# The sum of squares of three norms by four 32-column products, a copy and one product inside a column

## What is computed

```python
def rmsnorm(x, g):
    x32 = x.astype(jnp.float32)
    y = x32 * lax.rsqrt(jnp.mean(x32 * x32, axis=-1, keepdims=True) + EPS)
    return (y * g.astype(jnp.float32)).astype(x.dtype)
...
    a = rmsnorm(h, norm2[i])                                      # norm 2
    h = h + (jax.nn.silu(a @ w_gate[i]) * (a @ w_up[i])) @ w_down[i]
...
def sq_relu_mlp(h, w_up, w_down):
    return jnp.square(jax.nn.relu(h @ w_up)) @ w_down
...
    x = x + sq_relu_mlp(rmsnorm_2(x, mlp_norm[layer]), w_up[layer], w_down[layer])   # layer 0 and 1
```

## Time and profile before

| | |
|---|---|
| median of 3 runs | 887.29 us |
| lowest of them | 886.36 us |
| the profiled execution | 886.04 us, of it the span 884.3 us |
| granted TensorE clock, mean | 0.998 |
| TensorE busy | 868.6 us |
| weight loads | 837.4 us |
| VectorE busy | 607.5 us |
| ScalarE busy | 470.6 us |
| GpSimd busy | 95.0 us |

### The profile page before, as it was taken

How to read it: one execution, slowest core, us unless ns; L and a number is a source line. 1 busy time by engine, 2 the same in 40 slices (tenths; PEclk the granted TensorE clock), 3 DMA queues, 4 the chain that set the end, 5 groups by cost and what they waited for, 6 DMA issues and landing times.

```text
span 884.3 us, 19363 instructions
## 1 busy us (share of the span) xinstructions
PE 868.6 (98%) x7310; PEld 837.4 (95%) x7310; DVE 607.5 (69%) x994; ACT 470.6 (53%) x755; POOL 95.0 (11%) x139
## 2 busy tenths in 40 slices
PE   8999999999999999999999999999999999999996
PEld 8888899999999999787999999999999999999996
DVE  4766558666566587877866666668979966666665
ACT  6556666434444385448744444445786644444443
POOL 3420002000000029611100000001110100000001
PEclk9999999999999999999999999999999999999999
DMA  7532336665655648623465555555534565555551
GB/s 250 170 118 97 118 122 223 204 191 173 204 177 181 198 147 234 175 98 125 160 225 189 183 187 187 189 188 166 166 131 158 169 214 189 189 188 185 188 174 48
DMA packets 44434, 152.10 MB, mean 172 GB/s; under 512 B 5604, under 2 KB 6884, under 8 KB 44388
## 3 DMA queue, kind: packets, MB, share of 16 engines
q1 hardware_dynamic: 41184, 145.52, 50.3%
q0 software_dynamic: 2400, 4.89, 1.8%
q10 hardware_dynamic: 804, 1.04, 0.3%
HBM read 148.64 MB, written 1.05 MB: 169 GB/s over the span
## 4 chain that ended last, share of the span: by engine, by line
PE 87%; DVE 7%; ACT 3%; issue 1%; DMA 1%; SPq 0%; DVEq 0%; ACTq 0%
PE bank L1363 26%; PE bank L1365 26%; PE bank L1364 26%; DVE alo L953 2%; DVE wlo L929 2%; PE bank L1713 1%; PE bank L1397 1%; PE bank L1447 1%; PE bank L1492 1%; PE bank L1469 1%; PE bank L1803 1%; ACT whi L513 1%; DMA raw<-in_slabs 1%; DVE h L963 1%; PE bank L1391 1%
## 5 line engine op out<-in xcount | busy, mean ns | idle before, releaser
L1363 PE MATMUL bank<-ahi,whi 128*128 128x256 f32 (+1 forms) x1400 | 400.4, 286 | 1.9 <-DVE alo L947 1.2
L1364 PE MATMUL bank<-alo,whi 128*128 128x256 f32 (+1 forms) x1400 | 394.0, 281 | 0.0
L1365 PE MATMUL bank<-ahi,wlo 128*128 128x256 f32 (+1 forms) x1400 | 393.9, 281 | 0.0
L929 DVE TENSOR_TENSOR wlo<-raw,whi 128x1024 fp32r<-128x1024 f32 x273 | 332.2, 1225 | 30.3 <-ACT whi L513 30.2
L513 ACT ACTIVATE whi<-raw 128x1024 fp32r<-128x1024 f32 x273 | 282.4, 1051 | 93.1 <-PE bank L1365 83.4
L1363 PEld LDWEIGHTS bank<-ahi,whi 128*128 128x128 f32 x1400 | 264.0, 189 | 6.4 <-DVE alo L947 2.6
L1364 PEld LDWEIGHTS bank<-alo,whi 128*128 128x128 f32 x1400 | 264.0, 189 | 0.4
L1365 PEld LDWEIGHTS bank<-ahi,wlo 128*128 128x128 f32 x1400 | 264.3, 189 | 0.0
L1363 PE MATMUL bank<-hidhi,whi 128*128 128x256 f32 x704 | 195.1, 277 | 0.7 <-DVE hidlo L947 0.7
L1365 PE MATMUL bank<-hidhi,wlo 128*128 128x256 f32 x704 | 195.1, 277 | 0.0
L1364 PE MATMUL bank<-hidlo,whi 128*128 128x256 f32 x704 | 194.4, 276 | 0.0
(11 more groups left out here) (223 smaller groups left out, 724.4 us busy)
## 6 DMA issues: line engine op xcount, KB each, us to landing
raw<-in_slabs SPq DMA_DIRECT2D x273, 512.0 KB, 3.5
shared<-in_convw POOLq DMA_DIRECT2D x4, 512.0 KB, 6.8
shared<-zpad POOLq DMA_DIRECT2D x48, 35.5 KB, 3.6
raw<-in_slabs SPq DMA_DIRECT2D x8, 128.0 KB, 5.4
vtok<-in_gatew POOLq DMA_DIRECT2D x2, 512.0 KB, 5.4
out<-y SPq DMA_DIRECT2D x4, 256.0 KB, 2.8
h<-in_xT ACTq DMA_DIRECT2D x3, 272.0 KB, 5.2
h<-in_xT SPq DMA_DIRECT2D x1, 272.0 KB, 3.5
```

Source lines behind the costliest of these rows:

```text
L929: dve.tensor_tensor(wlo[:, n % R, :, :], raw[:, n % R, :, :], whi[:, n % R, :, :].bitcast(F32), ALU.subtract).then_inc(lo_done, 1)
L1363: pe.matmul(dst, hi, xh, start=start, stop=False, skip_group_check=True)
L1364: pe.matmul(dst, hi, xl, start=False, stop=False, skip_group_check=True)
L1365: return pe.matmul(dst, lo, xh, start=False, stop=stop, skip_group_check=True)
```

## The change

For the three norms `N_NORM2`, `N_MLP0` and `N_MLPC` (the table `PARTS`), the four products with 128 columns of ones are replaced. TensorE now multiplies each of GpSimd's four sums by 32 columns of ones, each product into 32 partitions of its own of half 1 of `stat_bank` (`stats_parts`). ScalarE copies the 128x256 result into `sq` 1 (`parts_factor`), and TensorE multiplies that copy once by the 128x128 ones (`stats_of_parts`). Each part then counts 32 times, so the logarithm's scale divides by 32 more. The one product stands inside the column of slab n+2, ahead of its fourth chunk (`column`, `amid`). On ScalarE the first of the two early splits (slab n+3) stays ahead of the norm, and the second (slab n+4) now follows the exponential. VectorE's and GpSimd's programs are the same.

```diff
--- before.py
+++ after.py
@@ -147,6 +147,8 @@
 
 (N_NORM1, N_NORM2, N_MIX0, N_MLP0, N_MIXC, N_MLPC, N_FINAL) = range(7)
 RS0 = (0, 1, 2, 4, 5, 6, 7)
+
+PARTS = (N_NORM2, N_MLP0, N_MLPC)
 
 SUMS = ((0, 2, 4, 6), (0, 2, 4, 6), (0, 6), (0, 2, 4, 6), (0, 6), (0, 2, 4, 6))
 SUM0 = (0, 4, 8, 10, 14, 16, 20)
@@ -292,6 +294,7 @@
         consts, gprod = sem("consts"), sem("gprod")
         h_ready, h_final = sem("h_ready"), sem("h_final")
         sq_ready, sum_ready, stat_ready, rstd_ready = sem("sq_ready"), sem("sum_ready"), sem("stat_ready"), sem("rstd_ready")
+        stat_parts, stat_copied = sem("stat_parts"), sem("stat_copied")
         plain_sq, plain_sum, plain_stat = sem("plain_sq"), sem("plain_sum"), sem("plain_stat")
         af_ready, ahi_ready, alo_ready = sem("af_ready"), sem("ahi_ready"), sem("alo_ready")
         act_hid, hid_hi, hid_lo = sem("act_hid"), sem("hid_hi"), sem("hid_lo")
@@ -563,8 +566,19 @@
                 return act.activation(dst, tmp, ACT.Exp, scale=-0.5)
 
             def norm_factor(i, src, lo=NMETA):
+
                 act.wait_ge(stat_ready, i + 1)
-                inverse_root(rstd[:, lo:], std[:, lo:], src, DM).then_inc(rstd_ready, 1)
+                inverse_root(rstd[:, lo:], std[:, lo:], src, DM * (32 if i in PARTS else 1)).then_inc(rstd_ready, 1)
+
+            def parts_factor(i, n):
+
+                if n - 1 in EARLY:
+                    split(n - 1 + LOOKAHEAD)
+                split(n + LOOKAHEAD)
+                act.wait_ge(stat_parts, PARTS.index(i) + 1)
+                act.activation(sq[:, 1, NMETA:], half(stat_bank, 1), ACT.Copy).then_inc(stat_copied, 1)
+                norm_factor(i, half(stat_bank, 0))
+                split(n + 1 + LOOKAHEAD)
 
             def operand_hi(s, f, k):
 
@@ -709,8 +723,7 @@
                 if u >= ROW1_SLOT and u + 1 < ROW1_SLOT + KC:
                     operand_hi(A_MIX1, F_MIX1, u + 1 - ROW1_SLOT)
             residual_hi(N_NORM2)
-            split_early(MLP1)
-            norm_factor(N_NORM2, stat_bank[:, 0:SEQ])
+            parts_factor(N_NORM2, MLP1)
 
 
             def swiglu(f, n, q=0, row=True):
@@ -821,8 +834,7 @@
             act.activation(lam[:, 2, :], lam[:, 1, :], ACT.Ln, bias=1.0).then_inc(lam_ln, 1)
             split_ahead(OUT2 + KC - 1)
             residual_hi(N_MLP0)
-            split_early(MLP2)
-            norm_factor(N_MLP0, stat_bank[:, 0:SEQ])
+            parts_factor(N_MLP0, MLP2)
 
 
             def squared_relu(f, n, e0, q=0, row=True):
@@ -903,8 +915,7 @@
             split_ahead(MLP3 - 1)
             exp_ln_tables()
             residual_hi(N_MLPC)
-            split_early(MLP3)
-            norm_factor(N_MLPC, stat_bank[:, 0:SEQ])
+            parts_factor(N_MLPC, MLP3)
             squared_relu_mlp(MLP3, E_MLP3)
             residual_hi(N_FINAL)
             for k in range(FINAL_D, KC):
@@ -1367,10 +1378,12 @@
             def slab_ready(n, q=0):
                 pe.wait_ge(lo_done, n + 1 + R * q)
 
-            def column(n, bank, q=0, lo=NMETA):
+            def column(n, bank, q=0, lo=NMETA, amid=None):
 
                 slab_ready(n, q)
                 for k in range(KC):
+                    if amid and k == 3:
+                        amid()
                     ins = three(bank[:, lo:T1], n, k, ahi[:, k, lo:], alo[:, k, lo:], k == 0, k == KC - 1)
                 ins.then_inc(slab_used, 1)
 
@@ -1446,6 +1459,19 @@
                     pe.wait_ge(sum_ready, SUM0[i] + j + 1)
                     ins = pe.matmul(dst, ones[:, :], sq[:, k, lo:], start=(j == 0), stop=(j == len(SUMS[i]) - 1))
                 ins.then_inc(stat_ready, 1)
+
+            def stats_parts(i):
+
+                for j in range(4):
+                    pe.wait_ge(sum_ready, SUM0[i] + j + 1)
+                    ins = pe.matmul(half(stat_bank, 1)[32 * j:32 * j + 32, :], ones[:, 0:32], sq[:, 2 * j, NMETA:],
+                                    start=True, stop=True, skip_group_check=True)
+                ins.then_inc(stat_parts, 1)
+
+            def stats_of_parts(i):
+
+                pe.wait_ge(stat_copied, PARTS.index(i) + 1)
+                pe.matmul(half(stat_bank, 0), ones[:, :], sq[:, 1, NMETA:], start=True, stop=True).then_inc(stat_ready, 1)
 
             def plain_stats():
 
@@ -1661,16 +1687,16 @@
                     operand_row(OUT1, A_MIX1, u - ROW1_SLOT)
 
 
-            def gate_up(f, n, q=0):
+            def gate_up(f, n, q=0, amid=None):
 
                 if f > 1:
                     pe.wait_ge(gemm_evac, E_MLP1 + 2 * f - 1 + 8 * q)
-                column(n, aux_bank if f == 1 else gemm_bank[0], 3 * q)
+                column(n, aux_bank if f == 1 else gemm_bank[0], 3 * q, amid=amid)
                 pe.wait_ge(gemm_evac, E_MLP1 + 2 * f + 8 * q)
                 column(n + 1, gemm_bank[1], 3 * q)
             first_columns(MLP1, A_NORM2)
-            stats(N_NORM2)
-            gate_up(1, MLP1 + 2)
+            stats_parts(N_NORM2)
+            gate_up(1, MLP1 + 2, amid=lambda: stats_of_parts(N_NORM2))
             hidden_row(0, MLP1 + 4, 0, first=True)
             with pe.Fori(0, (FF1 - 6) // 4) as it:
                 for j in range(4):
@@ -1765,8 +1791,8 @@
 
             def squared_relu_mlp(base, e0, m0, s, i):
                 first_columns(base, s)
-                stats(i)
-                column(base + 2, col_bank(2))
+                stats_parts(i)
+                column(base + 2, col_bank(2), amid=lambda: stats_of_parts(i))
                 hidden_row(0, base + 3, m0, first=True)
                 hidden_row(1, base + 4, m0 + 1)
```

## The result

| | before | changed |
|---|---|---|
| median | 886.40 us | 889.70 us |
| the profiled execution | 886.04 us | 889.05 us |
| span of it | 884.3 us | 887.3 us |
| TensorE busy | 868.6 us | 867.7 us |
| ratio of the times | | 1.0039, 95% interval 1.0028 to 1.0051 |

The changed kernel is slower by 3.3 us by the medians and 3.5 us by the ratio (one execution of either that was disturbed is left out of the ratio). That is 0.4%, no change by the 2% that the prediction named. A second timing beside a kernel of before at 885.99 us gave 889.58 us, ratio 1.0040 (1.0026 to 1.0054). TensorE is busy for 0.9 us less in a span that is 3.0 us longer.

The account below looks back on a forecast made before the run. TensorE, busy for 98% of the span, was taken to bound the kernel, plus its few waits. Costs of 0.93, 0.93 and 1.55 us at the three norms, 3.41 in all, on 886.04 gave 889.5 us; range 887.0 to 892.6.

Parts of the forecast that it names:

- Packing: At each norm, the four 32-column products run side by side on TensorE, 0.67 us with tile switches instead of 1.73.
- Rival 2: The four products don't run side by side and take 1.95 us; total 892.6 us; chance 0.08.
- the rule that the prediction set beside it: Weight loads overlap matmuls in flight only where row groups differ; column tiles share one, so the four products would run serially.
- The column moves up to T0+0.91 only: After the products TensorE is ready at T0+0.67, but the column waits for VectorE's slab low half until T0+0.91.
- T0: Start of the sums' products at each norm, from which the prediction gives all other times as distances in us.
- The copy hides: ScalarE's 0.385 us copy of the sums ends by T0+1.15, hidden by nine matmuls before the product at T0+1.97.
- The norm is late: At each norm the final sum is out at T0+2.59, 0.70 us later than before; at C the logarithm starts at T0+2.63.
- The split shows by 0.34 and 0.94: ScalarE's moved split delays the chain by 0.34 us at each squared-ReLU MLP and 0.94 us at the gated MLP.
- rival 3: The moved split on ScalarE hides; only the norm's lateness counts, 1.8 us over three places: 887.8 us; chance 0.12.
- First rows: First MLP output rows start at T0+5.50 (squared-ReLU, before 4.57) and T0+8.96 (gated, before 7.41), behind TensorE waits.
- rival 1: Waits on slab and chain prove shorter, so TensorE's 0.61 us saving a place comes off: 884.2 us; chance 0.04.
- rival 4: TensorE's clock falls in the new 1.3 and 1.6 us waits, costing up to 8 us more, 898 us; chance 0.03.

## Why the prediction was right

889.5 us was forecast and 889.7 measured; the cost was put at 3.41 us and measured at 3.3 and 3.6. That the totals agree to 0.2 us is in part chance, since the base of the sum, 886.04 us, lay 0.36 below the median that the kernel before then had. By its steps:

- *Packing.* The products and their tile switches were put at 0.67 us; 0.66 with the slab's wait taken away. The convolution's rows were the right ones. Rival 2 (no packing) falls: eight weight loads of 32 columns take 0.16 us in all and the eight matmul records start within 0.26 us. With it falls the rule that the prediction set beside it, by which column tiles would run one behind another; the measurement decides.
- *The column moves up to T0+0.91 only.* Load at T0+0.80 and matmul 0.10 behind it: 0.90. The weight load's own record names VectorE's low half, and with six matmuls that don't need it in front the load moved to T0+0.66.
- *The copy hides.* It runs from T0+0.80 to 1.19 and the product starts at T0+1.97: hidden as forecast. Ahead of the second chunk it shows by 0.09 us.
- *The norm is late.* Logarithm at T0+2.60, for 2.63; before it was 1.93. The product six matmuls earlier made the kernel faster by 1.5 to 1.8 us with the same work on TensorE.
- *The split shows by 0.34 and 0.94.* When it was put back the first row came 0.35 us earlier at the last MLP and 0.94 at the gated one. Over the three places putting it back gave 1.5 to 1.8 us and moving it alone cost 1.4 us, for 1.6 and 1.3 worked out, so rival 3 (the split hides) falls.
- *First rows.* T0+5.47 for 5.50 at the last MLP; at the gated one 149.12 - 140.20 = 8.92 for its record, where 8.96 was said for the matmul. By the distance of the starts the waits in front of them, forecast at 1.3 and 1.6 us, were 1.29 and 1.72, and the one in front of the gated MLP's second column, forecast at 0.3, was 0.29 (from 144.38 to 144.67). No second wait came behind either, as said.
- *The saving is kept* (rival 1) falls with the kernel whose product is early and whose split is out of the way: TensorE has the same saving there and the time is that of before. Its 1.83 us also supposes that the slab's wait goes; with that wait in place only 0.32 us a place could have shown there.
- *The clock* (rival 4) stayed at 1.00 in the waits.

I took one price too low: I let the 0.10 us load of the first matmul stand only where there is a wait. It is also there behind the switch of tiles (the first matmul of the column without the slab's wait has the longer record too). It did not change the sum, since the slab's wait came later. And the range was widened on its low side for the gap between base and median, which lies above the base and could only have made the time longer; the result lies well inside either way.

## What to carry to other kernels

Before making a product cheaper, look at when its result is wanted: here 0.21 us of slack stood between the norm's chain and the end of the column that hid it, and a form that needs 0.6 us less of TensorE's work but gives the result 0.7 us later was a loss at all three places. Whatever is put between the halves of a reduction (a copy, nine other matmuls, a wait for a slab) adds to the chain and takes from its cover at once. Work moved on an in-order engine out of an idle stretch and into the chain costs the part that no other link of the chain runs beside: 0.35 us of the split's 1.05 where VectorE evacuated meanwhile, 0.94 where a table load had to wait for it. And what a wait costs on TensorE is read from the distance of two starts: the record's own figure was 0.16 us short in both places looked at (1.03 for 1.19 and 0.16 for 0.32), and the first matmul's weight load, 0.10 us, comes on top.

## What the runs showed that I had not expected

With float32r output GpSimd's sums took no longer than before (0.74 us for the first of them at the last MLP in both kernels; the row of the kernel before stands below), and four single-pass products take 0.12 us each where float32 ones take 0.43, so this one change gave 2.0 to 2.4 us over the three norms.

```profile
694.63 0.74 POOL L390 TENSOR_TENSOR sq<-sq 128x256 f32<-128x256 f32 x1 [40.83 <-ACT sq L533]
```

And the wait for a slab's low half, worth 0.5 us over three places in the changed kernel, was worth 1.0 to 1.4 us once the sums were cheaper and the chain no longer in front: it had grown from 0.14 to 0.32 us, since TensorE came to it earlier. Taken away together with the first matmul's load, it let the column start 0.48 us behind the products' start instead of 0.79, and the first row came 0.43 us earlier at the last MLP. The middle place repeats that with 0.42 and the gated MLP gives 0.25, together 1.1 us by the starts of the records.
